# Expert outputs added in DRAM by accumulating scatters, weighted on the way out of PSUM

## What is computed

```python
x = x + merged @ w_out                       # the residual, y in the kernel
t = rms_norm(x, norm_ffn_w)
grp_p, grp_idx = top_k(softmax(t @ w_rg + b_rg), 1)
top_logits, top_local = top_k(in_group_logits, 2)
weights = grp_p * softmax(top_logits)        # two weights per token
for e in the two experts of a token:         # 16 experts, hidden width 256
    x = x + weight_e * ((silu(t @ w_gate[e]) * (t @ w_up[e])) @ w_down[e])
return rms_norm(x, norm_final_w)
```

## Time and profile before

| | us |
|---|---|
| median of 3 executions | 698.45 (696.98 to 699.14) |
| the profiled execution | 698.4 |
| its span, first to last instruction | 696.6 |
| PE busy | 643.5 (92%) |
| DVE busy | 471.2 (68%) |
| ACT busy | 396.8 (57%) |
| POOL busy | 173.6 (25%) |
| POOL's DMA queue | 8.43 MB, 12672 packets, 4.0% of 16 engines' span |

### The profile page before, as it was taken

The page is one execution under the profiler, slowest core; times in us unless marked ns, Lnnn a source line. Parts: engine busy times, 40 slices in busy tenths (PEclk is TensorE's granted clock), DMA queues, the critical chain, the costliest instruction groups (busy, mean ns, idle before and its releaser), DMA issues.

```text
span 696.6 us, 9255 instructions
## 1 busy us (share of the span) xinstructions
PE 643.5 (92%) x3375; PEld 537.6 (77%) x3376; DVE 471.2 (68%) x779; ACT 396.8 (57%) x673; POOL 173.6 (25%) x216
## 2 busy tenths in 40 slices
PE   4999999999999999999999997999999999998920
PEld 4788778788878888888888886788878887887810
DVE  4768995354631434424664548999999998998717
ACT  7428584255633432335352355479898898987623
POOL 7000007992000000000000001144545655445210
PEclk9999999999999999999999999799999999999975
DMA  8434334213222111111325816568788797866335
GB/s 276 153 95 87 61 80 132 77 60 76 62 65 62 61 61 60 62 61 61 121 68 214 323 44 206 173 209 277 225 269 264 217 306 245 280 215 221 100 145 235
DMA packets 73728, 104.63 MB, mean 150 GB/s; under 512 B 31633, under 2 KB 53202, under 8 KB 73554
## 3 DMA queue, kind: packets, MB, share of 16 engines
q1 hardware_dynamic: 60912, 95.57, 42.5%
q0 software_dynamic: 12672, 8.43, 4.0%
q10 hardware_dynamic: 98, 0.03, 0.0%
HBM read 123.90 MB, written 17.83 MB: 203 GB/s over the span
## 4 chain that ended last, share of the span: by engine, by line
PE 73%; DVE 14%; ACT 4%; DMA 4%; issue 2%; POOL 2%; SPq 0%; POOLq 0%; ACTq 0%; DVEq 0%
PE bank L1599 20%; PE bank L1601 19%; PE bank L1600 19%; DVE down_lo L1368 3%; DVE gate_up_lo L1368 3%; PE bank L1747 2%; DMA ew_raw<-in_w_gate,extra_weight_rows 1%; PE bank L2018 1%; DVE rank_onehot L1483 1%; PE bank L1657 1%; DVE unit_in_lo L1518 1%; DMA expert_rows<-expert_rows_hbm 1%; PE bank L1816 1%; PE bank L1806 1%; ACT unit_out L1004 1%
## 5 line engine op out<-in xcount | busy, mean ns | idle before, releaser
L1599 PE MATMUL bank<-h_hi,w_hi 128*128 128x512 f32 x304 | 124.5, 410 | 2.3 <-POOL sub_product L669 2.3
L1601 PE MATMUL bank<-h_hi,w_lo 128*128 128x512 f32 x304 | 119.7, 394 | 0.0
L1600 PE MATMUL bank<-h_lo,w_hi 128*128 128x512 f32 x304 | 119.7, 394 | 0.0
L1368 DVE TENSOR_TENSOR gate_up_lo<-ew_raw,gate_up_hi 128x1024 fp32r<-128x1024 f32 x92 | 108.3, 1218 | 9.6 <-ACT gate_up_hi L952 9.5
L693 POOL DMA_INDIRECT unit_tokens<-ffn_rows,row_index x23 | 30.5, 1327 | 297.7 <-DVE row_index L1491 285.9
L952 ACT ACTIVATE gate_up_hi<-ew_raw 128x1024 fp32r<-128x1024 f32 x92 | 92.2, 1057 | 9.8 <-DMA ew_raw<-in_w_gate,extra_weight_rows 8.8
L1053 DVE TENSOR_TENSOR w_lo<-w_raw,w_hi 128x2048 fp32r<-128x2048 f32 x26 | 60.1, 2312 | 49.9 <-ACT w_hi L746 49.9
L1599 PE MATMUL bank<-gate_up_hi,unit_in_hi 128*128 128x512 f32 x184 | 76.6, 416 | 0.0
L1601 PE MATMUL bank<-gate_up_hi,unit_in_lo 128*128 128x512 f32 x184 | 72.8, 396 | 0.0
L1600 PE MATMUL bank<-gate_up_lo,unit_in_hi 128*128 128x512 f32 x184 | 72.6, 394 | 0.0
L1599 PEld LDWEIGHTS bank<-h_hi,w_hi 128*128 128x128 f32 x304 | 57.9, 190 | 13.6 <-DVE w_lo L1066 2.5
(11 more groups left out here) (361 smaller groups left out, 1295.9 us busy)
## 6 DMA issues: line engine op xcount, KB each, us to landing
w_raw<-in_w_in SPq DMA_DIRECT2D x17, 1024.0 KB, 5.2
ew_raw<-in_w_gate SPq DMA_DIRECT2D x32, 512.0 KB, 6.3
ew_raw<-in_w_up SPq DMA_DIRECT2D x32, 512.0 KB, 5.8
ew_raw<-in_w_down SPq DMA_DIRECT2D x32, 512.0 KB, 5.0
w_raw<-in_w_out SPq DMA_DIRECT2D x4, 1024.0 KB, 5.0
expert_rows<-expert_rows_hbm SPq DMA_DIRECT2D x8, 512.0 KB, 6.9
x_T<-in_x SPq DMA_DIRECT2D x4, 512.0 KB, 5.1
w_raw<-in_w_in SPq DMA_DIRECT2D x8, 256.0 KB, 4.3
```

The lines of the kernel that those rows point to most:

```text
L1368: dve.tensor_tensor(dst, eraw[slot][:, :], hi.bitcast(F32), ALU.subtract).then_inc(elo_done, 1)
L1599: pe.matmul(out_ap, lhs_hi, rhs_hi, start=first, stop=False)
L1600: pe.matmul(out_ap, lhs_hi, rhs_lo, start=False, stop=False)
L1601: return pe.matmul(out_ap, lhs_lo, rhs_hi, start=False, stop=last)
```

## The change

The additions are moved into DRAM:

- After the residual is formed, SP stores each tile of y to a new DRAM tensor, `token_sums_hbm` (512 rows), ahead of the tile's `ffn_rows` store.
- The weights go into one tile `w12` (128 x 2 x 4) in place of w1 and w2; the last of the four operations signals WEIGHTS_SET. PE transposes it in unit 0, into bank 1, ACT copies it to SBUF behind its high parts of unit 1's rows, and stores it to `slot_weights_hbm` (1024 x 1) from its own queue. POOL gathers one weight per row of a unit (`weigh`) into a column of `uw`, three units ahead.
- `unit_out` multiplies by this column (the ACTIVATE's scale), after a wait for it.
- `spread` scatters to `token_sums_hbm` by token row (column 1 of `row_index`) with `compute_op=ALU.add`, and waits for the scatter before it to land (the first one for the residual stores).
- At the end SP loads four tiles of sums into y, ACT waits for these, and the eight DVE additions and the eight row loads are gone, as is the wait for `gu_ps`.

```diff
 h_rows = nc.dram_tensor("ffn_rows", (S, D), F32)
-o_rows = nc.dram_tensor("expert_rows_hbm", (2 * S, D), F32)
+sum_rows = nc.dram_tensor("token_sums_hbm", (S, D), F32)
+wt_rows = nc.dram_tensor("slot_weights_hbm", (2 * S, 1), F32)
...
@@ SP @@
             for t in range(TT):
+                sp.wait_ge(y_done, TT + t + 1)
+                sp.dma_start(sum_rows[t * P:(t + 1) * P, :], y[:, t, :]).then_inc(residual_out, 16)
                 if t < TT - 1:
...
-            sp.wait_ge(gu_ps, UNITS)
             for t in range(TT):
-                for k in range(2):
-                    sp.dma_start(pair[k][:, t, :], o_rows[S * k + t * P:S * k + (t + 1) * P, :]).then_inc(pair_in[t], 16)
+                sp.dma_start(y[:, t, :], sum_rows[t * P:(t + 1) * P, :]).then_inc(sums_in[t], 16)
...
@@ POOL @@
             def spread(u):
                 pool.wait_ge(ot_done, u + 1)
+                if u:
+                    pool.wait_ge(ot_out[(u - 1) % 2], 16 * ((u - 1) // 2 + 1))
+                else:
+                    pool.wait_ge(residual_out, 16 * TT)
                 nc.gpsimd.indirect_dma_start(
-                    out=o_rows[:, :], out_offset=bass.IndirectOffsetOnAxis(ap=ridx[:, SEQ[u], 0:1], axis=0),
+                    out=sum_rows[:, :], out_offset=bass.IndirectOffsetOnAxis(ap=ridx[:, SEQ[u], 1:2], axis=0),
                     in_=ot[u % 2][:, :], in_offset=None,
-                    bounds_check=2 * S - 1, oob_is_err=False).then_inc(ot_out[u % 2], 16)
+                    bounds_check=S - 1, oob_is_err=False, compute_op=ALU.add).then_inc(ot_out[u % 2], 16)
+
+            def weigh(u):
+                pool.wait_ge(ids_done, 1 + batch_of(SEQ[u]))
+                nc.gpsimd.indirect_dma_start(
+                    out=uw[:, u:u + 1], out_offset=None, in_=wt_rows[:, :],
+                    in_offset=bass.IndirectOffsetOnAxis(ap=ridx[:, SEQ[u], 0:1], axis=0),
+                    bounds_check=2 * S - 1, oob_is_err=False).then_inc(wt_in[u % 4], 16)
 
             for u in range(4):
                 fetch(u)
+            pool.wait_ge(wt_out, 16)
+            for u in range(3):
+                weigh(u)
             for u in range(UNITS):
+                if u + 3 < UNITS:
+                    weigh(u + 3)
                 if u + 4 < UNITS:
                     fetch(u + 4)
                 spread(u)
...
@@ ACT @@
             def unit_out(u):
                 act.wait_ge(dn_ps, u + 1)
+                act.wait_ge(wt_in[u % 4], 16 * (u // 4 + 1))
                 if u >= 2:
                     act.wait_ge(ot_out[u % 2], 16 * (u // 2))
                 for h in range(2):
-                    ins = act.activation(ot[u % 2][:, S * h:S * (h + 1)], ps[5 + h][:, :], ACT.Copy)
+                    ins = act.activation(ot[u % 2][:, S * h:S * (h + 1)], ps[5 + h][:, :], ACT.Copy, scale=uw[:, u:u + 1])
...
+                if u == 0:
+                    act.wait_ge(wt_turned, 1)
+                    act.activation(w12_f[:, :], ps[1][0:2 * TT, 0:P], ACT.Copy).then_inc(wt_turned, 1)
+                    act.wait_ge(wt_turned, 2)
+                    act.dma_start(wt_rows[:, :].rearrange("(r p) o -> r (p o)", p=P), w12_f[:, :]).then_inc(wt_out, 16)
...
-                act.wait_ge(tok_added, t + 1)
+                act.wait_ge(sums_in[t], 16)
...
@@ DVE, at the end @@
-            def add_experts(t):
-                dve.wait_ge(pair_in[t], 32)
-                link(dve.scalar_tensor_tensor(y[:, t, :], pair[0][:, t, :], w1[:, t:t + 1], y[:, t, :], ALU.mult, ALU.add))
-                dve.scalar_tensor_tensor(y[:, t, :], pair[1][:, t, :], w2[:, t:t + 1], y[:, t, :],
-                                         ALU.mult, ALU.add).then_inc(tok_added, 1)
...
-            add_experts(0)
-            for t in range(1, TT):
-                add_experts(t)
-                final_norm(t - 1)
-            final_norm(TT - 1)
+            for t in range(TT):
+                final_norm(t)
...
@@ PE, in the loop over units, after unit_in(u + 1) @@
+                if u == 0:
+                    pe.wait_ge(choice_step, WEIGHTS_SET)
+                    pe.transpose(ps[1][0:2 * TT, 0:P], w12[:, :, :].rearrange("p k t -> p (k t)"), ident[:, :]).then_inc(wt_turned, 1)
+                if u == 1:
+                    pe.wait_ge(wt_turned, 2)
```

More of the change, by code:

```diff
@@ L197, in build @@
         nffn = at("norm_ffn_b", [P, D], F32, r_tmp + 8192)
-        pair = [at(f"expert_rows{k}", [P, TT, D], F32, r_main + 16384 * k) for k in range(2)]
         out_t = at("out_T", [P, TT, D], F32, ffn_raw)
@@ L217, in build @@
         e1, e2, e12 = rt("first_onehot", [P, TT, EG]), rt("second_onehot", [P, TT, EG]), rt("both_onehot", [P, TT, EG])
-        m1, m2, dif, w1, w2 = (rt(n_, [P, TT]) for n_ in ("first_logit", "second_logit", "logit_gap", "first_weight", "second_weight"))
+        m1, m2, dif = (rt(n_, [P, TT]) for n_ in ("first_logit", "second_logit", "logit_gap"))
+        w12 = rt("slot_weights", [P, 2, TT])
         sel = rt("chosen", [P, TT, NG, EG])
@@ L286, in build @@
         brg = new("router_bias", [P, NG + NE])
+        w12_f = new("slot_weights_F", [2 * TT, P])
+        uw = new("unit_weights", [P, UNITS])
         row_rep = at("index_row_repeated", [P, P, 16], BF16, tri_at)
@@ L349, in build @@
         hid_hi, hid_lo, dn_ps, ot_done = sem("hidden_hi_done"), sem("hidden_lo_done"), sem("down_ps"), sem("unit_out_done")
-        pair_in = [sem(f"expert_rows_in{t}") for t in range(TT)]
-        tok_added = sem("y_added")
+        sums_in = [sem(f"token_sums_in{t}") for t in range(TT)]
+        residual_out, wt_turned, wt_out = sem("residual_rows_out"), sem("slot_weights_turned"), sem("slot_weights_out")
+        wt_in = [sem(f"unit_weights_in{i}") for i in range(4)]
         pool_set = sem("gpsimd_set")
@@ L356, in build @@
         choice_step = sem("choice_step")
-        GD_IN, ED_IN, SEL_DONE, EXPERTS_KNOWN = range(1, 5)
+        GD_IN, ED_IN, SEL_DONE, WEIGHTS_SET, EXPERTS_KNOWN = range(1, 6)
         choice_exp = sem("choice_exp")
@@ L635, in _ @@
             nc.gpsimd.memset(ones[:, :], 1.0)
+            link(nc.gpsimd.memset(uw[:, :], 0.0))
             link(nc.gpsimd.memset(tri[:, :], 1.0))
@@ L1507, in _ @@
             dve.wait_ge(choice_exp, ED_OUT)
[L1508 to L1511, removed]
+            link(dve.tensor_scalar(w12[:, 0, :], dif[:, :], 1.0, None, ALU.add))
+            link(dve.reciprocal(w12[:, 0, :], w12[:, 0, :]))
+            link(dve.tensor_tensor(w12[:, 0, :], w12[:, 0, :], gp[:, :], ALU.mult))
+            dve.tensor_tensor(w12[:, 1, :], w12[:, 0, :], dif[:, :], ALU.mult).then_inc(choice_step, 1)
             row_ids(4)
```

## The result

The changed kernel is slower: a median of 703.5 us (698.7 to 709.2, 20 runs) against 698.5 us (695.7 to 701.7, 20 runs) for the kernel before in the same session, a ratio of 1.0068 (95% interval 1.0050 to 1.0086).

A forecast was written before the change was run, and what follows sets the result against it. PE was taken as the bound (73% of the chain), with a serial tail bound by DVE after it. 698.4 - 8.5 (tail) + 4.2 (expert stage) = 694.1 us, range 688.5 to 702.5.

The forecast's parts named there:

- the lateness e of the extra gate loads: Expert stage: 0.18 us from the longer unit_out plus d, together 0.68 us, costing the stage +4.2 us.
- d: Expert stage: delay of extra gate loads by an accumulating scatter in front; 0.5 us taken, bounds 0 to 3.2.
- repeated traffic: Scatter's rows fetched again for adding: 1.1 us; half of it was taken as d.
- The price of lateness: Expert stage: five places feel e fully, two only beyond 0.26 us; in the second rival 7e - 0.5 us.
- The scatter's new wait: Expert stage: waiting for the scatter before costs nothing, as long as an accumulating one lands within about 9 us.
- The scatter's own a: Tail: extra time of the accumulating last scatter; 1.5 us taken, bounds 0 and 3.2.
- The tail: After the last scatter: -10.4 us from fewer loads and no additions, +1.5 scatter, +0.36 scaled evictions; sum -8.5 us.
- gathers, residual stores and the turned weights: Before and in the expert stage: expected to fit idle time or cover and cost nothing.
- The second one: Rival, slower: extra gate loads wait behind accumulated rows, d = 1.8, stage +13.3 us, total 703.2 us; chance 0.18.
- The first, a free accumulation: Rival: accumulation costs nothing in tail or queue; tail -10.0, stage +0.9, total 689.3 us; chance 0.2.
- The rule that I set aside: Expert stage: by it the gate load's semaphore waits for all accumulated rows, making d the scatter's whole extra time.
- the second rival: Slower case: extra gate loads wait behind the accumulated rows; 703.2 us, chance 0.18.

The follow-up runs named there:

- e6: Changed kernel plus an empty gather on POOL's queue behind the last scatter, with ACT and DVE marking the landings; one profile, 703.0 us.
- e7: Same markers as e6, but with plain scatters in place of accumulating ones (sums wrong); one profile, 693.4 us.
- e1: The changed kernel run again unaltered, for a yardstick and second profile; 702.2 us, ratio 1.006.
- e4: Changed kernel with the extra units' gate loads issued ahead of the scatter; 690.4 us, ratio 0.9892.
- e2: Changed kernel with plain scatters in place of accumulating ones (sums wrong); 694.0 us, ratio 0.9937.
- e3: Changed kernel without the gathers of weights and ACT's waits for them, scale set to 1.0; 701.9 us, ratio 1.0054.
- e9: Changed kernel plus 64 KB loads on SP's queue at the end, one issued 1.2 us behind the last scatter; one profile, 702.0 us.
- e11: Repeat of e4, on the same chip as e12; 691.3 us, ratio 0.9914.
- e12: Repeat of e5; 693.5 us, ratio 0.9945.
- e5: The kernel before the change, with only the extra units' gate loads moved ahead of the scatter; 693.4 us, ratio 0.9939.

## Why the prediction was wrong

**The step that failed** is "What remains is the lateness e of the extra gate loads": of its bounds 0 to 3.2 for d I took 0.5, because a gate load had landed before the scatter issued ahead of it, and because I took loads and scatter to share engines. e6 against e7 measures d as 2.3 us where nothing else runs. In the stage the seven waits grew by 7.6 us: 1.1 each on average, from 0.2 (0.89 against 0.67) to 2.1 (3.74 against 1.62), where I had e = 0.68. Both of my reasons fall by the record.

*The landing was not the one that ACT waits for.* The two halves of a gate load count on one semaphore (`extra_in[slot // 2]`, 16 each), and ACT starts only at the full count. What the earlier trace rows gives as the landing of the first half, 498.1, is the 16th signal of the two together, whichever half gave it. The one that counts is the second half's, still in the kernel before:

```profile
496.05 1.00 POOL L708 DMA_INDIRECT ew_raw<-in_w_gate,extra_weight_rows  x1 [0.30 <-DVE down_lo L1368]
...
DMA to landing us min/median/max: 3.1/3.1/3.1
```

It landed at 499.2, 0.4 us behind the scatter (498.8), and ACT started at 499.26. All seven gate pairs of the kernel before ended behind their scatter: 0.4 us behind it at the four waits of 1.5 us and more, 0.7 to 2.4 us at the three short ones. And at no moment had a pair given more than twice as many of its signals as the scatter ahead had given of its own. So nothing in these rows was out of order; they already agreed with what e6 shows.

*The loads share no traffic with the scatter, because they move no rows.* With this input all seven extra units are empty. POOL's queue made 12672 packets, 88 transfers of 144: 23 fetches, 23 scatters and 42 extra weight loads. Of its 8.43 MB, 8.39 are the 1024 rows of 4 KB fetched and the 1024 scattered. A stretch that holds the packets of an empty unit's scatter and of the last extra unit's two down loads (647.5 to 652, the DMA view of the kernel before) shows 432 packets, three times 144, with no bytes:

```profile
q0 software_dynamic: 432, 0.00, 4.6%
```

So the "repeated traffic" from which I took d could not reach them; what was late was their signal alone.

**The price of lateness was right.** 7e - 0.5 with the measured mean e of 1.09 is 7.1 us. The stage took 9.9 + 1.7 = 11.6. What is left, some 4.5 us, is what I set at nothing:

- The clock of TensorE, which I did not cost: 1.6 us. Behind PE's longest gap (2.65 us) the twelve down products took 4.41 us, at a mean granted clock of 0.61, part of it at the lower of the two levels (1.2 GHz). The same twelve took 2.85 us behind the gap of 2.53. Two stretches of e1 (columns as in the earlier trace rows):

```profile
507.93:510.78 2.85, 2.85 (x12) 2.34 (x13) 2.85 (x4) 2.45 (x4) 0.66 (x1) 1.00 0.82 234
597.37:601.78 4.41, 4.41 (x12) 3.35 (x13) 4.41 (x5) 2.44 (x4) 0.65 (x1) 0.61 0.76 252
```

  From unit 6 to unit 22 the granted clock fell nowhere else in e1, and nowhere in the kernel before or in e4.
- The scatter's new wait: "nothing, as long as an accumulating one lands within about 9 us". One landed after 9.7 us, and the next scatter, with the extra down loads behind it, was held some 3.5 us; PE then waited 1.1 us for down_lo (at 669.53). The landing was not worked out: before the change the longest took 7.7 us and the last one gained 3.0. And 9 us was too wide a limit there: the scatter of 648.63 was itself late, so the next one could have gone 7 us after it.
- The extra down loads, also behind a scatter, which I did not cost: 2.3 to 4.1 us of waiting.

How the last 1.8 us divide was not separated.

**The scatter's own a** was 3.0 us, not 1.5; it lies within the bounds (0 to 3.2). I priced the repeated traffic (1.1 us) and expected the rest to overlap. e1 beside e2 shows the transfer three times as long (3.5 us against 1.2) and POOL 0.6 us longer, together close to the upper end, the whole trip of a read. The plain transfer itself took 1.2 us in the kernel before as well, not the 1.7 that I read there. Why the accumulating one is so long was not separated.

**The tail** otherwise went as worked out: 14.2 us from the last scatter's landing (685.96) to the end against 14.1 predicted, four loads, no addition on DVE, pairs of scaled evictions of 1.26 to 1.27 us. With a = 3.0 its sum is -7.0 instead of -8.5, and -7.1 was measured. That gathers, residual stores and the turned weights cost nothing held (e3; unit 6 starts 0.9 us earlier in e1 than before, 0.1 and 0.4 later in e4 and e2).

**The rivals.** The second one happened: it gave 703.2 us with d = 1.8, and the runs gave 703.5 and 702.2. That it came so close is in part luck. Its stage was 1.7 us too long (13.3 against 11.6) and its tail 1.4 us too good (-8.5 against -7.1), and the seven waits grew by a mean of 1.09 us where it had e = 1.98; the clock and the new wait, which it did not have, made up for that. The first, a free accumulation at 689.3, is e2 in substance: its tail (19.7 us from the last `unit_out`, 9.8 less than before) is as worked out, its stage is 1.7 us above that of the kernel before where I had 0.9, and its median of 694.0 lies higher than its profiled execution (690.9).

**The rule that I set aside.** By the Trainium skill, DMA: Bandwidth & Descriptors, section "Queues, rings and completion order", a semaphore increment lands only after every earlier write of that DMA engine, across its queues. Within POOL's queue e6 agrees with it (signal 0.16 us behind the scatter's), and so do the seven gate pairs of the kernel before. Across queues no run shows it: in e9 SP's load signalled 3.4 us ahead of the earlier scatter. That does not refute it either. In e1 the last scatter's rows moved from 2.1 to 5.6 us after its issue, and in e9 SP's load had signalled 3.5 us after the scatter's issue, so much of the scatter may have been written after the load. I should have given the rule the weight of the rows that agreed with it, the longest waits just where the scatter ahead had landed late, which the prediction lists as "for" the second rival and then outweighs by one misread landing.

**What stays open**: the trace does not say which of the 16 DMA engines gave which signal, so that each engine signals POOL's transfers in their order is a reading of the counts, and nothing here shows how a load with rows of its own would fare. Also open is why the granted clock fell behind the gap of 2.65 us and not behind that of 2.53. It fell in e11 too, where PE had waited only 1.92 us: the last twelve down products took 4.60 us at a mean granted clock of 0.63, against 3.03 us at 1.00 in e12. That is 1.6 us by which e11's profiled execution gains less over e12's (3.6 us of span) than tail and stage would give. e4's profiled execution (688.4) is 2.0 us below its median and e5's (692.6) 0.8 below, so the 4.1 us between their spans (686.7 and 690.8) overstate the change by about 1.2. How often the clock falls in the executions that were not profiled is not known.

The best of these kernels is e4, the change with the gate loads ahead of the scatter: 690.4 and 691.3 us, 7.9 and 6.7 us below the kernel before.

## What to carry to other kernels

On a queue that issues in program order, making one transfer slower makes all those behind it late; look at what stands behind it and how much cover that has left before counting what the transfer saves elsewhere. Put the urgent loads ahead of a slow scatter, but only those that have nothing to wait for, since everything behind them inherits that wait. Before reading a landing, look which semaphore count the consumer waits for: when two transfers count on one semaphore, the moment when the first half of the count is reached need not be the landing of the first transfer. And look whether a transfer moves any rows before pricing what its traffic meets.

## What the runs showed of the hardware

- A scatter with addition of some 78 rows of 4 KB (0.32 MB) took POOL 1.6 us in place of 1.0, moved for 3.5 us in place of 1.2 (e1, e2), and landed 6.2 us after its issue in place of 3.2 (kernel before); in the stage, up to 9.7 us (10.4 in the first profile of the changed kernel).
- An empty gather behind it on the same queue signalled after 4.6 us in place of 2.3.
- The seven pairs of empty gate loads of the kernel before ended 0.4 to 2.4 us behind the plain scatter ahead of them on the same queue, never before it.
- The granted TensorE clock fell for part of twelve products behind a gap of 2.65 us (mean 0.61, 4.41 us in place of 2.85; e1) and not behind one of 2.53 (1.00).
- A 64 KB load on SP's queue issued 1.2 us after the accumulating scatter overtook it by 3.4 us, and signalled as fast (2.3 us) as beside a plain scatter (2.5).
